# A gated-linear-attention and dilated-window layer: inputs by single tiles with DMA transposes, cache copies over before the samples, the mixer's third z moved, and its last tile with column halves side by side

## The reference

```python
xn = _rmsnorm(x, g_pre); u = xn @ w_in                     # 1024 -> 10256 columns
gq, gk, gv, gg, glr, dq, dk, dv, dg, ga, gb = split(u)
y_a = (rmsnorm(gla(gq, gk, gv, glr)) * silu(gg)) @ w_gla_branch          # 1024 x 1024
y_b = (softmax-weighted sum of three dilated windows(dq, dk, dv) * silu(dg)) @ w_dil_branch   # 512 x 1024
merged = sigmoid(ga) * y_a + sigmoid(gb) * y_b
h = x + _rmsnorm(merged @ w_out, g_post)
y = h + (pe @ w_ple_proj) * sigmoid(h @ w_ple_gate)
```

## Time and profile before

| | us |
|---|---|
| median of 3 runs | 2875.69 |
| profiled execution | 2874.96 |
| its span | 2873.2 |
| TensorE busy | 2824.2 (98%) |
| VectorE busy | 1077.1 (37%) |
| ScalarE busy | 873.7 (30%) |
| GpSimd busy | 375.7 (13%) |
| DMA, mean | 192 GB/s |

### The profile page before, as it was taken

The page is one execution under the profiler, slowest core; times in us unless marked ns, Lnnn a source line. Parts: engine busy times, 40 slices in busy tenths (PEclk is TensorE's granted clock), DMA queues, the critical chain, the costliest instruction groups (busy, mean ns, idle before and its releaser), DMA issues.

```text
span 2873.2 us, 41107 instructions
## 1 busy us (share of the span) xinstructions
PE 2824.2 (98%) x16336; PEld 1490.4 (52%) x16336; DVE 1077.1 (37%) x2416; ACT 873.7 (30%) x1791; POOL 375.7 (13%) x609
## 2 busy tenths in 40 slices
PE   7999999999999999999999989999999999999998
PEld 4444455665545665566555545555544444444444
DVE  4211134444332443344223323343323455555532
ACT  5201023444322322333123321111113444444431
POOL 0000010101222001130011023332200000000000
PEclk9999999999999999999999999999999999999999
DMA  6234444545468565574476769898846965665541
GB/s 210 90 116 134 142 163 158 200 168 196 161 231 285 171 201 183 186 238 159 169 264 221 220 174 328 282 307 279 273 166 197 282 176 161 169 170 148 152 107 33
DMA packets 293992, 550.80 MB, mean 192 GB/s; under 512 B 153453, under 2 KB 158389, under 8 KB 289817
## 3 DMA queue, kind: packets, MB, share of 16 engines
q1 hardware_dynamic: 242746, 289.37, 33.0%
q0 software_dynamic: 51056, 258.81, 27.2%
HBM read 378.05 MB, written 236.67 MB: 214 GB/s over the span
## 4 chain that ended last, share of the span: by engine, by line
PE 93%; DMA 3%; DVE 2%; SPq 1%; issue 1%; ACT 1%; POOL 0%; DVEq 0%; POOLq 0%
PE out L2475 41%; PE out L2082 21%; PE out L2472 14%; PE out L1072 2%; PE out L1057 2%; PE out L2478 2%; PE out L1063 1%; PE out L568 1%; PE out L578 1%; PE out L579 1%; PE out L1352 1%; PE out L1048 1%; PE out L1312 1%; DMA sw_rows<-U 1%; DMA sw_kc<-in_cache_kv_w 1%; PE out L543 1%
## 5 line engine op out<-in xcount | busy, mean ns | idle before, releaser
L2475 PE MATMUL out<-w_hi,xn_hi 128*128 128x512 f16 x1920 | 729.2, 380 | 0.0
L2475 PE MATMUL out<-w_lo,xn_hi 128*128 128x512 f16 x1920 | 728.7, 380 | 0.0
L2475 PE MATMUL out<-w_hi,xn_lo 128*128 128x512 f16 x1920 | 728.6, 379 | 0.0
L2387 ACT ACTIVATE stage<-out 128x512 f32<-128x512 f32 (+1 forms) x170 | 99.4, 585 | 914.9 <-PE out L2475 657.6
L2419 DVE TENSOR_SCALAR stage<-out 128x512 f32<-128x512 f32 (+1 forms) x170 | 114.9, 676 | 627.1 <-PE out L2475 457.1
L2475 PEld LDWEIGHTS out<-w_hi,xn_lo 128*128 128x128 f16 x1920 | 188.1, 98 | 227.2 <-issue 1.1
L2475 PEld LDWEIGHTS out<-w_hi,xn_hi 128*128 128x128 f16 x1920 | 188.7, 98 | 205.3 <-issue 6.8
L2475 PEld LDWEIGHTS out<-w_lo,xn_hi 128*128 128x128 f16 x1920 | 188.2, 98 | 201.3 <-issue 0.8
L2472 PE MATMUL out<-xn_hi,w_hi 128*128 128x512 f16 x640 | 242.8, 379 | 2.2 <-DVE w_lo L2358 2.1
L2472 PE MATMUL out<-xn_hi,w_lo 128*128 128x512 f16 x640 | 242.6, 379 | 0.0
L2472 PE MATMUL out<-xn_lo,w_hi 128*128 128x512 f16 x640 | 242.6, 379 | 0.0
(11 more groups left out here) (307 smaller groups left out, 4056.4 us busy)
## 6 DMA issues: line engine op xcount, KB each, us to landing
out<-in_cache_kv_w POOLq DMA_DIRECT2D x64, 1020.0 KB, 8.8
U<-stage SPq DMA_DIRECT2D x240, 256.0 KB, 5.1
raw<-in_w_in SPq DMA_DIRECT2D x80, 512.0 KB, 5.1
sw_kc<-in_cache_kv_w POOLq DMA_DIRECT2D x24, 1024.0 KB, 13.7
sw_vc<-in_cache_kv_w POOLq DMA_DIRECT2D x24, 1024.0 KB, 9.8
UT<-stage SPq DMA_DIRECT2D x80, 256.0 KB, 3.0
sw_rows<-U POOLq DMA_DIRECT2D x32, 512.0 KB, 9.6
out<-in_cache_kv_w POOLq DMA_DIRECT2D x16, 1008.0 KB, 9.6
```

The source lines that it names most:

```text
L2387: move_out(act, m, lambda o, x: act.activation(o, x, ACT.Copy, scale=1.0 / W_SCALE))
L2475: last = pe.matmul(out[m % 3][:, :], x[:, k, at:at + P], y[:, k, :], start=first, stop=final)
```

## The change

1. Input tiles are handled singly, in a ring of eight x buffers. Tiles 0 to 3 are transposed by TensorE, two of them before the first matmul; tiles 4 to 16 are scaled, split in rows to upper and lower half, and turned by two DMA transposes each on SP's queue, in the slots of tile t - 3. The gains come as a broadcast 128x1024 tile and are multiplied in with the scale. All four weight pieces of the first column tile have buffers of their own. The first column tile is now one of GV, stored as it is.
2. Cache copies: two in slots 6 and 14 of a column tile, one in 22 and 30, six to a tile.
3. Samples start one slot later; the steps of keys and queries, the flip and the turn of probabilities come one slot later in the period, the value product does not; the values of the first sample are loaded two slots after its start.
4. The mixer's third z is prepared in the last projection slot, 679, behind that slot's move out. Weights of gate's upper half are loaded together with those of out.
5. The mixer's last tile is held as 128 x 512: columns 0 to 511 on partitions 0 to 63, the others on 64 to 127. Its pairs of matmuls write the two partition halves of one bank. The partial means are exchanged by two small DMAs and added.

```diff
-ORDER = ([U_GQ, U_GK, U_GV, U_GV + BANK]
+ORDER = ([U_GV, U_GQ, U_GK, U_GV + BANK]
          + [column + g * WIDTH for g in range(GROUPS) for column in (U_DQ, U_DK, U_DV)]
          + [U_GG, U_GG + BANK, U_DG, U_GA, U_GA + BANK, U_GB, U_GB + BANK])
 TURNED = [U_GQ, U_GK] + [U_DQ + g * WIDTH for g in range(GROUPS)]
...
-SAMPLE_SLOT, SAMPLE_PERIOD = 526, 15
+SAMPLE_SLOT, SAMPLE_PERIOD = 527, 15
...
+    RING = 8
+    FIRST = 4
+    UNITS = FIRST * SLOTS
...
+    def load(self, sp, t):
+        if t >= self.RING:
+            self.wait_read(sp, t - self.RING)
+        src = self.x_sample.rearrange("b t d -> (b t) d") if t == TOKEN_TILES - 1 else self.x_prompt[0, t * P:(t + 1) * P, :]
+        sp.dma_start(self.tile(t), src).then_inc(self.x_loaded[t % self.RING], 16)
+
+    def load_g(self, sp):
+        sp.dma_start(self.g[:, :], self.g_pre.to_broadcast([P, D_MODEL])).then_inc(self.g_loaded, 16)
...
+    def square(self, act, t):
+        rows = self.rows(t)
+        act.wait_ge(self.x_loaded[t % self.RING], 16 * (t // self.RING + 1))
+        wait(act, self.squared, t - 1)
+        act.activation(self.squares[t % 2][:rows, :], self.tile(t), ACT.Square, scale=D_MODEL ** -0.5,
+                       accum_out=self.mean[:rows, t:t + 1]).then_inc(self.squared, 1)
+
+    def norm(self, pool, t):
+        rows = self.rows(t)
+        pool.wait_ge(self.squared, t + 1)
+        apart(pool)
+        pool.tensor_scalar(self.guarded[:rows, t:t + 1], self.mean[:rows, t:t + 1], NORM_EPS, None, ALU.add).then_inc(self.guarded_ready, 1)
+        pool.wait_ge(self.guarded_ready, t + 1)
+        pool.tensor_tensor(self.rstd[:rows, t:t + 1], self.guarded[:rows, t:t + 1], self.power[:rows, :], ALU.pow).then_inc(self.rstd_ready, 1)
+
+    def scale(self, dve, t):
+        if t == 0:
+            dve.wait_ge(self.g_loaded, 16)
+        dve.wait_ge(self.rstd_ready, t + 1)
+        dve.scalar_tensor_tensor(out=self.tile(t), in0=self.tile(t), scalar=self.rstd[:self.rows(t), t:t + 1], in1=self.g[:self.rows(t), :],
+                                 op0=ALU.mult, op1=ALU.mult).then_inc(self.scaled, 1)
+
...
+    def turn(self, pe, t):
+        rows = self.rows(t)
+        pe.wait_ge(self.scaled, t + 1)
+        for c in range(SLOTS):
+            n, bank, ks, _ = self.place(t, c)
+            wait(pe, self.lo_ready, n + 1 - len(self.bank))
+            for j, k in enumerate(range(ks.start, ks.stop)):
+                last = pe.transpose(bank[:, j, :], self.tile(t)[:, k * P:(k + 1) * P], self.identity[:rows, :rows])
+            last.then_inc(self.turned, 1)
+
...
+    def wait_read(self, sp, t):
+
+        if t < self.FIRST:
+            sp.wait_ge(self.turned, (t + 1) * SLOTS)
+        else:
+            sp.wait_ge(self.row_lo, t - self.FIRST + 1)
+
+    def wait_turned(self, eng, t):
+
+        n = t - self.FIRST
+        eng.wait_ge(self.row_turned[n % 2], 32 * (n // 2 + 1))
+
+    def wait_all(self, eng):
+        eng.wait_ge(self.lo_ready, self.UNITS)
+        for t in range(TOKEN_TILES - 2, TOKEN_TILES):
+            self.wait_turned(eng, t)
+
+    def split_hi(self, act, t):
+        n, rows = t - self.FIRST, self.rows(t)
+        act.wait_ge(self.scaled, t + 1)
+        if n >= 2:
+            self.wait_turned(act, t - 2)
+        act.activation(self.row[n % 2][0][:rows, :], self.tile(t), ACT.Copy).then_inc(self.row_hi, 1)
+
+    def split_lo(self, dve, t):
+        n, rows = t - self.FIRST, self.rows(t)
+        dve.wait_ge(self.row_hi, n + 1)
+        dve.tensor_tensor(self.row[n % 2][1][:rows, :], self.tile(t), self.row[n % 2][0][:rows, :], ALU.subtract).then_inc(self.row_lo, 1)
+
+    def turn_rows(self, sp, t):
+        n, rows = t - self.FIRST, self.rows(t)
+        sp.wait_ge(self.row_lo, n + 1)
+        for part, xn in enumerate((self.xn_hi, self.xn_lo)):
+            sp.dma_start_transpose(xn[:, :, t * P:t * P + rows], self.row[n % 2][part][:rows, :]).then_inc(self.row_turned[n % 2], 16)
 
     def scalar(self, act, slot):
+        t, half = divmod(slot, SLOTS)
+        if half == 1:
+            if t + 2 < self.FIRST:
+                for c in range(SLOTS):
+                    self.keep_hi(act, t + 2, c)
+            if t == 0:
+                self.square(act, 4)
+            if self.has(t + 5):
+                self.square(act, t + 5)
+        elif t + 3 >= self.FIRST and self.has(t + 3):
+            self.split_hi(act, t + 3)
 
     def vector(self, dve, slot):
+        t, half = divmod(slot, SLOTS)
+        if half == 1:
+            if t + 2 < self.FIRST:
+                for c in range(SLOTS):
+                    self.keep_lo(dve, t + 2, c)
+            if t + 3 < self.FIRST:
+                self.scale(dve, t + 3)
+            if self.has(t + 4):
+                self.scale(dve, t + 4)
+        elif t + 3 >= self.FIRST and self.has(t + 3):
+            self.split_lo(dve, t + 3)
 
     def tensor(self, pe, slot):
+        t, half = divmod(slot, SLOTS)
+        if half == 1 and t + 2 < self.FIRST:
+            self.turn(pe, t + 2)
+
+    def queue(self, sp, slot):
+        t, half = divmod(slot, SLOTS)
+        if half == 1 and t + 3 >= self.FIRST and self.has(t + 3):
+            self.turn_rows(sp, t + 3)
+        if half == 0 and self.has(t + self.RING):
+            self.load(sp, t + self.RING)
+
+    def wait_half(self, pe, t, half):
+
+        if t < self.FIRST:
+            pe.wait_ge(self.lo_ready, t * SLOTS + half + 1)
+        elif half == 0:
+            self.wait_turned(pe, t)
 
...
-    FREED_SLOTS = {0: 3, 1: 4, 2: 5, 3: 9, 4: 5}
+    FIRST = 1
+    FLIP_SLOT = FIRST + EVERY * (STEPS - 1) + 1
+    VALUE_SLOT = 12
+    FREED_SLOTS = {0: 3, 1: 4, 2: 6, 3: 10, 4: 5}
...
-            self.load_v(q, 0)
         self.queue_rows(q, r)
         c, u = divmod(r, SAMPLE_PERIOD)
         if 0 <= c < DEC_BATCH - 1:
                     self.load_k(q, c + 1, p)
             if u == 2:
                 self.load_q(q, c + 1)
-            if u == 13:
+                if c == 0:
+                    self.load_v(q, 0)
+            if u == self.VALUE_SLOT + 1:
                 self.load_v(q, c + 1)
-        if 0 <= c < DEC_BATCH and u == 13:
+        if 0 <= c < DEC_BATCH and u == self.VALUE_SLOT + 1:
...
-        if at == 0 and i < self.STEPS:
+        i, at = divmod(u - self.FIRST, self.EVERY)
+        if at == 0 and 0 <= i < self.STEPS:
             x = c * self.STEPS + i
             _, place, j, first = self.step_of(x)
...
-    PREPARE_SLOT = LOAD_SLOT + 12
+    PREPARE_SLOT = LOAD_SLOT + 11
     TURN_SLOT = PREPARE_SLOT + 4
     PRODUCT_SLOT = TURN_SLOT + 6
     NEXT_SLOT = PRODUCT_SLOT
     MERGE_SLOT = NEXT_SLOT + 3
-    THIRD_SLOT = MERGE_SLOT + 4
+    THIRD_SLOT = COLUMN_TILES * TILE_SLOTS - 1
...
+    def beside(self, t):
+
+        return t == self.TILES - 1
+
+    def wide(self, t):
+        return BANK if self.beside(t) else D_MODEL
+
+    def half(self, t, banks, n):
+
+        if self.beside(t):
+            part = slice(n * BANK // 2, (n + 1) * BANK // 2)
+            return banks[0][:, part], part
+        return banks[n][:, :], slice(n * BANK, (n + 1) * BANK)
+
+    def places(self, t, dram, tile):
+
+        if not self.beside(t):
+            return [(dram, tile[:, :])]
+        return [(dram[:, c * BANK:(c + 1) * BANK], tile[c * SAMPLES:(c + 1) * SAMPLES, :BANK]) for c in range(2)]
+
...
-        sp.dma_start(self.gb[:rows, :], self.U[at, U_GB:U_GB + D_MODEL]).then_inc(self.gates_loaded.sem, 16)
+        at = self.at(t)
+        for column, tile in ((U_GA, self.ga[t % 2]), (U_GB, self.gb)):
+            for src, dst in self.places(t, self.U[at, column:column + D_MODEL], tile):
+                sp.dma_start(dst, src).then_inc(self.gates_loaded.sem, 16)
 
...
     def store(self, sp, t):
         after(sp, self.y_ready, t + 1)
-        sp.dma_start(self.prompt_or_sample(t, self.y_prompt[0], self.y_sample), self.x[t % 3][:self.rows(t), :]).then_inc(self.y_stored[t % 3].sem, 16)
+        for dst, src in self.places(t, self.prompt_or_sample(t, self.y_prompt[0], self.y_sample), self.x[t % 3]):
+            sp.dma_start(dst, src).then_inc(self.y_stored[t % 3].sem, 16)
+
+    def swap_means(self, sp):
+
+        t = self.TILES - 1
+        after(sp, self.m_step, t * 3 + 1)
+        for c in range(2):
+            sp.dma_start(self.other_mean[c * SAMPLES:(c + 1) * SAMPLES, :], self.mean_m[(1 - c) * SAMPLES:(2 - c) * SAMPLES, 0:1]) \
+              .then_inc(self.means_swapped.sem, 16)
 
...
         self.load_weights(sp, "out", self.w_hi, self.cut_hi)
         self.load_weights(sp, "out", self.w_lo, self.cut_lo)
+        self.load_weights(sp, "gate", self.w_hi, self.cut_hi)
...
             self.queue_last_weights(sp)
         if self.has(t - 1):
+            if self.beside(t - 1):
+                self.swap_means(sp)
             self.turn_h(sp, t - 1)
...
+        if self.beside(t):
+            after(pool, self.means_swapped, 32)
```

(73 more changed lines are left out.)

283 lines of the change are left out of this document (125 added, 158 removed).

## The result

The changed kernel takes 2831.79 us (median of 4 runs, 2829.74 to 2833.0), the kernel before, beside it on the same chip, 2874.61 (2873.28 to 2880.13). The ratio is 0.9847, 95% interval 0.983 to 0.9864. The forecast was 2834 with a range of 2821 to 2850.

A forecast was written before the change was run, and what follows sets the result against it. TensorE was taken as the bound, busy 98% of 2873.2 us. Gains of 18.3 + 4.8 - 1.5 + 19.8 = 41.4 off 2874.96 gave 2833.6, plus 0.7: 2834 us, with an 8-in-10 range of 2821 to 2850.

The forecast's parts named there:

- A, the start: Start of the first column tile: the first output tile needs two x tiles instead of four, ends at 20.0, gain 8.3 us.
- A, the rest: First column tile after tile 0: most transposes leave TensorE's stream, gain 12.0 us, with 2 us of waits allowed.
- rival 1: The first column tile's DMA queue is the bound: nine tiles each 0.5 to 1.5 us longer, 2838 to 2847; chance 0.15.
- The Trainium skill: Input transposes: its rule of transpose DMAs at ordinary speed would make the result 2 us lower; forecast sided with the trace.
- B: Samples: 2.6 us from starting one slot later plus 2.2 at the score sums, gain 4.8, bounds 0 and 12.
- part A: First column tile, inputs handled by single tiles: gain 18.3 us in all, bounds 10 and 21.
- The 2.2 for the sums: Samples: the queue freed of cache copies removes 2.2 of the 2.7 us TensorE waits for score sums.
- B, the mechanism: First sample: second key block's load lies behind three broadcast row loads at 162 GB/s; wait becomes 9.3 us, clock falls to 0.50.
- C: Mixer entry, third z and gate's weights: a 7.3 us wait for w_out replaces 4.8; net 1.5 slower, bounds 7 faster, 5 slower.
- Rival 5: Mixer entry: the third z and gate's weights gain what the wait shows, 6.7 us instead of -1.5: 2826; chance 0.12.
- D: Mixer's last tile, the samples': matmul pairs on column halves run side by side; gain 19.8 us, bounds 8 and 21.
- rival 4: Mixer's last tile: halves do not run side by side, each pair 0.43, gain 1 us, time 2853; chance 0.05.

The follow-up runs named there:

- e_turn3: The changed kernel with a third DMA transpose (upper half again, into a spare tile) for each of tiles 4 to 16: 2847.89 us.
- e_copies: The changed kernel with the cache copies spread as before, five to a column tile: 2832.77 us.
- e_v_back: The changed kernel with the first sample's values loaded again right behind its keys, before it starts: 2833.69 us.
- e_rows_behind: The changed kernel with the first sample's three broadcast row loads issued behind its key blocks: 2824.19 us.
- e_late3: The changed kernel with the samples three slots later, their first loads left in place, the mixer's first z prepared 8 instead of 11 slots after its loads: 2822.35 us.
- e_both_back: The changed kernel with the mixer's third z and the load of gate's upper half put back where they were before: 2829.92 us.
- e_split: The changed kernel with w_out loaded in four pieces and its product started when the first two have landed: 2833.76 us.
- e_hfree: The changed kernel with the samples' h turned into the half of mT that the last tile leaves free: 2827.99 us.
- e_unpack: The changed kernel with the mixer's last tile as before, 64 rows by 1024 columns, products not side by side: 2853.63 us.

## Why the prediction was right, step by step

- **A, the start.** Tile 0 was to be over at 20.0. Its move out starts at 20.11, VectorE's first scale, which waits for the gains, at 8.81, between the bounds of 7.3 and 9.2; the first matmul at 14.44 (13 to 15 forecast):

```profile
8.81 2.48 DVE L291 SCALAR_TENSOR_TENSOR x<-x,rstd,g 128x1024 f32<-128x1024 f32 x2 [8.81 <-DMA g<-in_g_pre]
```

- **A, the rest.** From the end of tile 0 (moved out at 28.36 and 20.11, 8.3 gained) to the end of the column tile 10.8 are gained; the forecast had 12.0 less 2 us of waits. The waits were 0.9, all at tile 7, which lasts 6.3 us, above the 5.5 that the forecast named as a sign of being wrong; the other tiles from 4 to 15 stay below it (one run; the scatter of the start, 4 us over twelve traces, is larger than any error in A). The queue just kept pace, as "5.0 of 5.2 us" has it, but it was full until 80 us and not only to tile 8; e_turn3 shows how near rival 1 was: with one transpose more per tile the queue is the bound.
- **The Trainium skill** ("Advanced Engine Details and Errata", X-Bar Transpose (TRN2)) has transpose DMAs as fast as ordinary ones. e_turn3 disagrees as the trace of before did: 256 KB in 1.6 us, or in 1.15 if only the waits are counted, is 160 to 230 GB/s (an estimate), beside 420 for ordinary loads.
- **B.** The term was short by 2.2. The slot was to give 2.6, and the traces bear it out: TensorE starts the last transposes ahead of the second key block at 1693.11 instead of 1709.62, which is 16.5 earlier where part A gave 19.1: it comes there 2.6 later by position. But the block also landed 1.1 earlier by position (TensorE goes on at 1701.97 instead of 1722.20, 20.2 earlier), which the forecast did not have and which lies within the scatter of 1.7 between runs: luck. The 2.2 for the sums were put down to the copies; e_copies shows that these do nothing, and e_v_back that at the first sample it is the values' load, which the forecast had only cleared of delaying the keys. Compared slot by slot, the 7.0 are 4.0 in the two slots of the key block (its wait 3.7), 1.8 at the first sample's sums and 1.2 over the other seven samples. Which edit gave the 1.2 is not settled: the steps on VectorE, retimed by one slot, were not undone alone, and of the kernel before there is one trace.
- **B, the mechanism.** That the broadcast rows in front of the second key block make the stall held: without them it is gone (e_rows_behind), and it is a matter of time between issue and landing (e_late3). As forecast, the clock is at its lower level (1.2 GHz) after it; in e_late3 it is not. Windows of the changed kernel, then of e_late3:

```profile
1700.00:1704.00 4.00, 2.03 (x7) 1.30 (x8) 0.00 (x0) 0.88 (x2) 0.00 (x0) 0.50 1.03 410
```

```profile
1700.00:1710.00 10.00, 10.00 (x87) 6.21 (x89) 5.19 (x6) 2.17 (x4) 1.58 (x3) 1.00 1.16 466
```

- **C.** Forecast -1.5, measured -1.0. The wait for w_out is 7.0 where 7.3 was put. TensorE comes to z(2)'s first product at 2219.31 instead of 2242.73, 23.4 earlier where 26.1 had been gained: 2.7 lost, forecast 3.3. 1.7 come back by tile 15's merge, forecast 1.6 for h(0). Rival 5 (the wait's 6.7 are gained) is out by e_both_back. e_split shows the mechanism further than the forecast had it: the last store of U behind the weights bounds this stretch as much as w_out does.
- **D.** 17.9 instead of 19.8. The pairs did what was said (rival 4 is out); the wait for h(16) was mis-sized by 0.8 (2.3 instead of 1.5), and the lower clock behind it, 8 x 0.215 = 1.7 us, was left out (in three of ten traces it is not there). e_hfree gets both back, 3.8 us.
- The errors of B (+2.2), D (-1.9), A (+0.8) and C (+0.5) cancel in part, and that is luck: the total was 1.7 from the profile, with terms that were up to 2.2 off.

## What to carry to other kernels

Look up the same instruction in both traces at every border of a stage: a wait that vanished (4.8 us here) can be worth less than nothing, since the next landing decides. Before a queue is given more work, sum its time per period against the period; at 5.0 of 5.2 us one more transpose per tile made the stage 15.8 us longer here. A small store that others wait for belongs ahead of the large loads, and a load that is needed at a fixed time ahead of broadcasts.

## What the runs showed of the hardware

- One more DMA transpose of 128 x 1024 f16 per tile in a full queue makes each of ten tiles 1.6 us later, 1.15 of it waits; the last three are hidden (e_turn3).
- Broadcast row loads fill the engines at 0.87 to 0.99 with 162 to 175 GB/s, where key blocks bring 311 to 379 (e_rows_behind).
- In the changed kernel the pairs of 64-row products behind the wait of 2.3 us run at 2.4 GHz from 2815.4 to 2816.5 and at 1.2 GHz until 2819.8. In six other traces the same happens, in three the same pairs behind waits of 2.3 to 2.5 us keep the full clock, and in e_unpack the single 64-row products behind a wait of 3.0 us keep it too, 60 in 13.15. So neither the length of the wait nor the pairs alone decide it; what does stays open.
- The same load, issued at the same place, let TensorE wait between 7.5 and 9.2 us in nine traces.
